# Wider band matmuls in the two pool mixers of a four-layer trunk, and another order of VectorE's first steps behind them

## The reference

```python
POOL_WINDOWS = (2, 4, 8, 16)        # one group of 256 features each

def trailing_mean(xg, win):
    cs0 = pad(cumsum(xg, axis=1), ((0, 0), (1, 0), (0, 0)))
    lagged = pad(cs0, ((0, 0), (win, 0), (0, 0)))[:, 1:L + 1]
    count = minimum(arange(1, L + 1), win)
    return (cs0[:, 1:] - lagged) / count

def pool_mixer(h, w, b, scale):     # h is the normed input
    for g, win in enumerate(POOL_WINDOWS):
        hg = h[..., g * POOL_GROUP:(g + 1) * POOL_GROUP]
        groups.append(trailing_mean(hg, win) - hg)
    mixed = einsum('blgc,gcd->blgd', stack(groups, axis=2), w)
    return (mixed + b) * scale
```

## Time and profile before

| | |
|---|---|
| median of three runs | 2133.59 us |
| the profiled execution | 2133.68 us |
| its span, first to last instruction | 2132.0 us |
| mean granted TensorE clock over the span | 0.979 |
| DVE, ACT, POOL busy | 76%, 40%, 11% of the span |

### The profile page before, as it was taken

One profiled execution on the slowest core, in us unless ns is written; L12 is line 12 of the kernel. 1 busy time (PEld: TensorE's weight loads), 2 busy tenths in 40 slices (PEclk: granted clock), 3 DMA queues, 4 the chain that ended last, 5 costly groups with the idle time before them and its releaser, 6 DMA issues.

```text
span 2132.0 us, 40406 instructions
## 1 busy us (share of the span) xinstructions
PE 2065.2 (97%) x15868; PEld 1992.8 (93%) x15868; DVE 1617.2 (76%) x2291; ACT 851.5 (40%) x1269; POOL 244.5 (11%) x364
## 2 busy tenths in 40 slices
PE   7999999999998899999999999999999989999997
PEld 6999999988886899999999999999999988989996
DVE  5797779667775579777879896588887867977794
ACT  6343334344443234333445444343433343433341
POOL 4000000502221500000050000200000041000003
PEclk8999999999997999999999999999999989999999
DMA  5323333331121223333331110224423422333332
GB/s 159 125 85 99 98 98 95 103 97 55 50 69 30 60 80 110 88 98 97 105 95 41 50 49 21 80 80 119 118 73 101 119 75 62 97 99 98 98 98 91
DMA packets 306744, 184.83 MB, mean 87 GB/s; under 512 B 6634, under 2 KB 303595, under 8 KB 306372
## 3 DMA queue, kind: packets, MB, share of 16 engines
q1 hardware_dynamic: 304764, 175.08, 28.7%
q10 hardware_dynamic: 1192, 4.34, 0.5%
q0 software_dynamic: 672, 3.80, 0.5%
HBM read 179.44 MB, written 6.44 MB: 87 GB/s over the span
## 4 chain that ended last, share of the span: by engine, by line
PE 80%; DVE 7%; DVEq 5%; issue 4%; ACT 2%; DMA 1%; SPq 0%; POOL 0%; POOLq 0%; ACTq 0%
PE ps L795 42%; PE ps L1050 32%; DVEq L2388 3%; DVE cv L2389 1%; PE ps L1185 1%; PE ps L893 1%; PE ps L1209 1%; DVE w_lo L1800 1%; DVEq L2373 0%; ACT z_hi L1510 0%; ACT h L1498 0%; PE ps L1390 0%; PE ps L809 0%; DVEq L2398 0%; DVE w_lo L2022 0%
## 5 line engine op out<-in xcount | busy, mean ns | idle before, releaser
L795 PE MATMUL ps<-hid_hi,w_hi 128*128 128x264 f32 (+1 forms) x1232 | 284.3, 300 | 1.7 <-DVE hid_lo L2078 1.7
L1050 PE MATMUL ps<-t_lo,y_hi 128*128 128x264 f32 (+1 forms) x1008 | 285.7, 283 | 0.0
L1050 PE MATMUL ps<-t_lo,w_hi 128*128 128x264 f32 (+1 forms) x1008 | 285.7, 283 | 0.0
L1050 PE MATMUL ps<-t_hi,w_lo 128*128 128x264 f32 (+1 forms) x1008 | 285.4, 283 | 0.0
L1050 PE MATMUL ps<-t_hi,y_lo 128*128 128x264 f32 (+1 forms) x1008 | 285.3, 283 | 0.0
L1050 PE MATMUL ps<-t_hi,w_hi 128*128 128x264 f32 (+1 forms) x1008 | 285.1, 283 | 0.1
L1050 PE MATMUL ps<-t_hi,y_hi 128*128 128x264 f32 (+1 forms) x1008 | 284.8, 283 | 0.0
L795 PE MATMUL ps<-hid_lo,w_hi 128*128 128x264 f32 (+1 forms) x1232 | 283.6, 300 | 0.0
L795 PE MATMUL ps<-hid_hi,w_lo 128*128 128x264 f32 (+1 forms) x1232 | 283.1, 299 | 0.0
L1565 ACT ACTIVATE w_hi<-w_raw 128x1024 fp32r<-128x1024 f32 (+1 forms) x108 | 127.8, 1201 | 328.1 <-PE ps L795 192.5
L795 PE MATMUL ps<-y_hi,w_hi 128*128 128x264 f32 (+1 forms) x1088 | 245.2, 302 | 12.8 <-DVE cv L2361 4.9
(11 more groups left out here) (277 smaller groups left out, 4417.2 us busy)
## 6 DMA issues: line engine op xcount, KB each, us to landing
w_raw<-in_ffn_w_gate SPq DMA_DIRECT2D x88, 512.0 KB, 5.0
w_raw<-in_ffn_w_up SPq DMA_DIRECT2D x88, 512.0 KB, 4.6
w_raw<-in_ffn_w_down SPq DMA_DIRECT2D x64, 512.0 KB, 4.3
w_raw<-in_ffn_w_down SPq DMA_DIRECT2D x32, 384.0 KB, 4.4
w_raw<-in_attn_w_qkv SPq DMA_DIRECT2D x16, 512.0 KB, 3.8
w_raw<-in_conv_w_in SPq DMA_DIRECT2D x16, 512.0 KB, 4.2
w_raw<-in_attn_w_qkv SPq DMA_DIRECT2D x16, 256.0 KB, 2.8
w_raw<-in_attn_w_o SPq DMA_DIRECT2D x8, 512.0 KB, 3.8
```

The source lines that it names most:

```text
L795: mm = pe.matmul(ps[:, bank + hf, 0:half], w[:, slot, col:col + P], x(hf), start=begin and w is m.w_hi and n == 0, stop=end and w is m.w_lo)
L1050: mm = pe.matmul(ps[:, bank, 0:hw], w[:, at:at + P], b[:, t, k, 0:hw], start=k == 0 and n == 0, stop=k == 3 and n == 2)
```

## The change

Two edits. In `windows` the column ranges of tiles 1, 3 and 4 become as wide as the bank's part that they write to; the matmuls read the zeros that `bands` has beside its band and add them. In VectorE's `pool_layer` the first steps behind `z_lo` are written in another order.

```diff
@@ windows
-                for i, out, c0, c1 in ((1, low, P, CUT), (2, high, 0, WIDE), (3, high, OVER + P - CUT - 1, CUT), (4, high, WIDE - LAST, WIDE)):
+                for i, out, c0, c1 in ((1, low, 0, CUT), (2, high, 0, WIDE), (3, high, 0, WIDE), (4, high, 0, WIDE)):
@@ pool_layer, on VectorE
-                for d in range(NB):
-                    if d < 2:
-                        split_lo(tile0 + 4 + d, 0, 0, cols[tile0 + 4 + d])
+                add_windows(0)
+                split_lo(tile0 + 4, 0, 0, cols[tile0 + 4])
+                y_lo(0, yn, row, 0, TOK)
+                split_lo(tile0 + 5, 0, 0, cols[tile0 + 5])
+                add_windows(1)
+                for d in range(2, NB):
                     add_windows(d)
-                    if d > 0:
-                        y_lo(d - 1, yn, row, 0, TOK)
+                    y_lo(d - 1, yn, row, 0, TOK)
                 y_lo(NB - 1, yn, row, 0, TOK)
```

## The result

The changed kernel takes 2135.89 us (median of 20 runs, 2133.61 to 2139.17); the kernel before, run beside it, 2132.61 us (20 runs, 2128.75 to 2134.47). The ratio is 1.0016 with a 95% interval of 1.001 to 1.0022: slower by 2.1 to 4.7 us. The forecast was +2.8 us and 2136.4. It started from the 2133.59 of three runs, 1 us above the 20 runs of before beside the result, so part of its closeness to 2135.89 is luck: the difference was 3.3 us in the medians.

A forecast was written before the change was run, and what follows sets the result against it. The prediction took both pool mixers as bound by PE from their first L795 on, and by VectorE only ahead of it in pool0. Pool0 +0.3 + 0.95 and pool3 +1.5 gave +2.8 us, 2136.4 us; range 2129.2 to 2140.5.

The forecast's parts named there:

- The block: Step for one padded `windows` block at the fast clock: +0.19 us, 1.61 instead of 1.42 us.
- all columns are paid: Rival for the padded blocks: all 992 added columns cost time, 0.41 us a block; 2139.2 us, chance 0.10.
- Thirteen blocks on the path: Step for uncovered padded blocks at 0.19 us each: five in pool0, 0.95 us, and eight in pool3, 1.5 us.
- pool3: Step for the layer 3 mixer: padding adds 1.5 us, the order changes nothing, PE runs without a gap.
- The start: Step for PE's first L795 in pool0: second w_lo waits for POOL's add, start at 44.57, +0.3 us.
- the second rival: In pool0 POOL stays out, PE starts 0.8 us earlier and the clock is held; 2132.3 us, chance 0.17.
- The clock: Step for both mixers' slow stretches at 1.2 GHz: clock rises at the same moment, so padding keeps its fast price.
- the likeliest case: Main forecast for both mixers: +2.8 us, 2136.4 us, own range 2135.0 to 2138.0, chance 0.36.
- Rival 3: In both mixers padding keeps the clock up, -4.7 us, 2128.9 us; chance 0.14.
- The first rival: In pool0 the clock stays low a round and a half longer, 3.5 us; 2139.9 us, chance 0.18.

The follow-up runs named there:

- e3: Kernel before with only tile 4 (32 rows) padded to the new column range; ratio 1.0005 to before.
- e4: Kernel before with only tiles 1 and 3 padded to the new column ranges; ratio 1.0 to before.
- e9: Kernel before with four more matmuls in each block that add only zeros, in both mixers; ratio 1.002 to before.
- e6: Changed kernel (padding and order) with ScalarE's square of block 0 made later, behind y_hi(1), in both mixers; ratio 1.0003 to before.
- e10: Kernel before with the padding alone, VectorE in the old order, run once more; ratio 1.0005 to before.
- e8: The changed kernel itself, nothing altered, eleven more runs; ratio 1.0011 to before.
- e1: Kernel before with the padding alone, VectorE in the old order; ratio 1.0006 to before.
- e2: Changed kernel with the old column ranges, so VectorE's new order alone; ratio 1.0002 to before.
- e5: VectorE's new order without padding, plus ScalarE's square of block 0 made later, behind y_hi(1), in both mixers; ratio 0.9989 to before.

## Why the prediction was right, step by step

- **The block.** Predicted 1.61 us, measured 1.64, and "all columns are paid" is refused by e3 and e4, 0.12 + 0.09 us against 0.41. The predicted bound, the longer of the columns and the load's 0.11, fits where full tiles follow one another (0.12 to 0.13 us). By tile the sums hold, within a tile they don't:

| us from start to start, first and second matmul of the tile | before | predicted | measured |
|---|---|---|---|
| tile 1 | 0.15, 0.11 | as before | 0.21, 0.12 |
| tile 2 | 0.18, 0.13 | as before | 0.12, 0.13 |
| tile 3 | 0.07, 0.20 | +0.07 together | 0.13, 0.22 |
| tile 4 | 0.13, 0.19 | about 0.14, 0.29 | 0.22, 0.22 |

  The first padded matmul of tile 1 and that of tile 4 are followed after 0.21 and 0.22 us, twice the bound. That is what a load (0.11) and the columns (0.11) make one behind the other, and the 0.13 of 32 columns and 0.15 of 128 come near it too; this is a reading of the numbers that no run tests. That what tile 1 lost was won back behind tile 2 and that tile 4's two errors cancel is luck, and makes the sum better than its terms.
- **Thirteen blocks on the path.** 13 x 0.21 = 2.7 us of PE. The eight of pool3 were predicted at 1.5 us and lengthen it by 1.6 in six profiles; e9 supports that such time reaches the end. That the pad costs twice as much at the slow clock was wrong, it is 0.33 us against 0.21. That the first three blocks of pool0 are covered holds in both profiles of the changed kernel, but not in e6 and e10, where the clock fell earlier.
- **The start.** Forecast +0.3 us at 44.57, with y_lo(0) at 41.4 and a second w_lo of 2.3 us; measured 44.36, 41.30 and 2.33. h(0) began at 39.48 and not at 39.6. But block 0 itself began 0.45 us earlier here (36.40, before 36.85), and that differs from profile to profile whatever the kernel, 36.4 to 37.1. Counted from block 0, PE's start is at 7.96 us, in e8 at 7.72, and before at 7.40. But part of that is the last z_lo, which came late in these two for want of ScalarE's z_hi, as it did in e1 with the old order. Counted from the start of the last z_lo, PE starts after 6.59 us before, 6.71 with the order alone (e2) and 6.84 in both profiles of the changed kernel: +0.25, half of it with the order alone, which leaves the other half to the padding in block 0. The forecast +0.3 is right. e5 shows POOL's add as the cause, by taking it away. Of the second rival this leaves its first half: with POOL out, PE starts 1.0 us earlier than before, but the clock is not held.
- **pool3.** I had expected no gap from its first block to its last run. In this profile there is one: the clock was still fast at block 0, so PE came to the last tile early and waited 0.81 us. It costs little: block 0 takes 2.83 us with the wait and took 2.68 before, and the mixer is no longer than in the other padded profiles (26.1 us).
- **The clock.** I had it unchanged in the likeliest case, and gave 0.14 to padding that keeps it up. Taken apart, it is a share and not a case: in the padding alone the loss is 2.2 to 2.9 us less, which by the fitted 0.6 gives back 1.3 to 1.7 us, most likely in pool0. In the changed kernel the loss is only 0.5 ± 0.6 and 1.1 ± 0.6 us less, so the sum of PE's time and the start, 2.7 + 0.25 with the measured sizes, stands nearly whole, and the forecast +2.8 lies in the measured 2.1 to 4.7. That is in part luck: nothing in the prediction says why the clock should give back less with the new order than without it, and no run here settles it; the difference, 1 to 2.4 us, is about two of its standard errors. Rival 3 also has a slip that moves no number: 480 of the added columns have 32 rows, not 544. The first rival (a round and a half more of slow clock in pool0) was not seen in either profile of the changed kernel.

## What to carry to other kernels

Padding short matmuls is not free and not paid by the column: read the pace of the weight loads, count only the columns beyond it, and look at the tile beside which the number of rows changes. A step moved ahead on one engine also moves what that step sets off on others; here it brought GpSimd's add onto the next VectorE instruction and gained nothing, and moving one square on ScalarE brought PE's start 1.0 us forward. Where the clock falls and rises inside a kernel, note time and mean granted clock of every run, fit how much of the one goes with the other before you subtract it, and look in the trace of each stage for what the mean can't tell.

## What the runs showed of the hardware

- A GpSimd add gets in between two VectorE instructions that stand ready, and the second, with both its inputs in SBUF, waits: w_lo takes 2.33 us with an add of 1.3 to 1.5 us ahead of it and 1.22 without (e2, e5), and ends 1.08 us behind the add's end.
- Behind a change of the number of rows (127 to 32, 32 to 128) the next matmul starts 0.19 to 0.22 us after the one before, where full tiles of 272 columns take 0.13 (after, e3, e4). The full sum of the padding is +0.21 us a block at 2.4 GHz and +0.33 at 1.2 GHz.
- Four more matmuls of 240 zero columns cost PE 0.50 us a block at 2.4 GHz, with 0.11 to 0.16 us from one to the next (e9), and thirty-two more of them in each mixer lower what is lost to the clock: 40.7 ± 0.6 us against 43.9 ± 0.2.
- One kernel's runs differ by up to 8.3 us on the same chip for the kernel before (35 runs) and 11.9 for e6 (12 runs), with a mean granted clock from 0.976 to 0.983 over all runs that goes with the time (the correlation is -0.6 to -0.9 in every set of runs). A difference of 1 us needs the clock beside it.
